# Raw tokens turned first, parameters loaded in two parts, other banks and another ScalarE order in attention, routing by column halves, and a last norm that ScalarE shares

## What is computed

```python
def hybrid_layer(x, ...):                      # first block, two layers
    h = rmsnorm(x, g_pre_mix)
    proj = h @ w_in                            # 16 pieces: heads of four kinds
    o_a = dsa_attention(...)                   # top 64 keys by an indexer
    o_b = forgetting_attention(...)            # decay by cumulated log gates
    o_c = differential_attention(...)          # lam = exp(lq1.lk1)-exp(lq2.lk2)+init
    o_d = sliding_window_sink_attention(...)
    x = x + rmsnorm(mix @ w_out, g_post_mix)
    m = jnp.square(jax.nn.relu(rmsnorm(x, g_pre_mlp) @ w_up)) @ w_down
    x = x + rmsnorm(m, g_post_mlp)
    return x + jax.nn.sigmoid(x @ w_ple_gate) * (p_i @ w_ple_proj)
```

## Time and profile before

| quantity | value |
|---|---|
| median of the three runs | 2034.21 us |
| the profiled execution | 2033.9 us |
| its span | 2032.1 us |
| busy PE / VectorE / ScalarE / GpSimd | 1988.8 / 1584.7 / 1210.5 / 96.9 us |
| share of PE in the chain that ended last | 93% |
| mean rate of the DMA queues | 237 GB/s |

### The profile page before, as it was taken

How to read it: one execution, slowest core, us unless ns; L and a number is a source line. 1 busy time by engine, 2 the same in 40 slices (tenths; PEclk the granted TensorE clock), 3 DMA queues, 4 the chain that set the end, 5 groups by cost and what they waited for, 6 DMA issues and landing times.

```text
span 2032.1 us, 30372 instructions
## 1 busy us (share of the span) xinstructions
PE 1988.8 (98%) x11719; PEld 1683.8 (83%) x11719; DVE 1584.7 (78%) x1636; ACT 1210.5 (60%) x1293; POOL 96.9 (5%) x162
## 2 busy tenths in 40 slices
PE   8999999999999999999999999999999999999996
PEld 7778888877888888888889888888888888888885
DVE  7777754778774469785458968989899999999998
ACT  5565534556554356544335636777777777777774
POOL 0310000031000000000000000000000000000000
PEclk9999999999999999999999999999999999999998
DMA  8316555532555554165556308999999999999994
GB/s 295 130 53 204 193 197 189 202 119 69 202 187 188 200 197 150 40 199 186 180 170 205 125 2 328 362 359 368 361 369 360 362 368 360 367 366 364 365 362 179
DMA packets 154216, 481.58 MB, mean 237 GB/s; under 512 B 14616, under 2 KB 41728, under 8 KB 153984
## 3 DMA queue, kind: packets, MB, share of 16 engines
q1 hardware_dynamic: 150048, 465.45, 63.8%
q0 software_dynamic: 4064, 14.68, 2.1%
HBM read 478.00 MB, written 2.10 MB: 236 GB/s over the span
## 4 chain that ended last, share of the span: by engine, by line
PE 93%; DVE 4%; ACT 1%; issue 1%; DMA 1%; POOL 0%; SPq 0%; DVEq 0%; POOLq 0%
PE G L673 18%; PE G L675 18%; PE G L674 18%; PE Sp L673 5%; PE Sp L675 5%; PE Sp L674 5%; PE G L1114 3%; PE G L700 3%; PE G L660 2%; PE G L1115 2%; PE G L655 1%; PE G L656 1%; PE Sp L1114 1%; PE G L1492 1%; DVE e_lo L2821 1%; PE G L978 1%
## 5 line engine op out<-in xcount | busy, mean ns | idle before, releaser
L1999 ACT ACTIVATE e_hi<-e_raw 128x1408 fp32r<-128x1408 f32 x384 | 524.1, 1381 | 154.7 <-DMA e_raw<-in_moe_w_gate 57.6
L2821 DVE TENSOR_TENSOR e_lo<-e_raw,e_hi 128x1408 fp32r<-128x1408 f32 x384 | 601.7, 1619 | 18.3 <-ACT e_hi L1999 15.5
L2071 DVE TENSOR_TENSOR ring_lo<-ring,ring_hi 128x2048 fp32r<-128x2048 f32 (+2 forms) x171 | 383.4, 2253 | 184.1 <-ACT ring_hi L1579 182.7
L1579 ACT ACTIVATE ring_hi<-ring 128x2048 fp32r<-128x2048 f32 (+1 forms) x179 | 335.4, 1882 | 228.6 <-PE G L675 132.2
L673 PE MATMUL G<-e_hi,xgTh 128*128 128x512 f32 (+1 forms) x768 | 289.5, 377 | 0.1
L675 PE MATMUL G<-e_hi,xgTl 128*128 128x512 f32 (+1 forms) x768 | 288.5, 376 | 0.0
L674 PE MATMUL G<-e_lo,xgTh 128*128 128x512 f32 (+1 forms) x768 | 286.9, 374 | 0.0
L673 PE MATMUL G<-ring_hi,xT 128*128 128x512 f32 (+2 forms) x500 | 195.7, 391 | 0.0
L675 PE MATMUL G<-ring_hi,xT 128*128 128x512 f32 (+2 forms) x500 | 192.1, 384 | 0.0
L674 PE MATMUL G<-ring_lo,xT 128*128 128x512 f32 (+2 forms) x500 | 191.9, 384 | 0.0
L674 PEld LDWEIGHTS G<-e_lo,xgTh 128*128 128x128 f32 x768 | 144.3, 188 | 23.8
(11 more groups left out here) (433 smaller groups left out, 3351.5 us busy)
## 6 DMA issues: line engine op xcount, KB each, us to landing
e_raw<-in_moe_w_gate SPq DMA_DIRECT2D x128, 704.0 KB, 6.0
e_raw<-in_moe_w_up SPq DMA_DIRECT2D x128, 704.0 KB, 6.0
e_raw<-in_moe_w_down SPq DMA_DIRECT2D x128, 704.0 KB, 6.0
ring<-in_w_in SPq DMA_DIRECT2D x48, 1024.0 KB, 5.1
ring<-in_w_mlp_up SPq DMA_DIRECT2D x32, 1024.0 KB, 5.2
ring<-in_w_mlp_down SPq DMA_DIRECT2D x32, 1024.0 KB, 4.8
ring<-in_w_out SPq DMA_DIRECT2D x16, 1024.0 KB, 4.9
ring<-in_ffn_w_gate SPq DMA_DIRECT2D x22, 512.0 KB, 3.8
```

The lines of the kernel that those rows point to most:

```text
L1579: nc.scalar.activation(ring_hi[:, n % H, 0:m], ring[:, n % R, 0:m], ACT.Copy).then_inc(w_hi.sem, 1)
L1999: nc.scalar.activation(e_hi[:, u, :], e_raw[:, u, :], ACT.Copy).then_inc(w_hi.sem, 1)
L2071: v.tensor_tensor(ring_lo[:, n % R, cs], ring[:, n % R, cs], ring_hi[:, n % H, cs].bitcast(F32), ALU.subtract).then_inc(w_lo.sem, 1)
L2821: v.tensor_tensor(e_lo[:, u, :], e_raw[:, u, :], e_hi[:, u, :].bitcast(F32), ALU.subtract).then_inc(w_lo.sem, 1)
```

## The change

Start. The raw tokens are turned as soon as they are there; the gain comes as eight rows of 128, is turned by PE to a column for each of the eight groups of features, and VectorE multiplies the turned tokens by it from PSUM (`gained`). ScalarE takes the high part of that product. The scale by the root is applied where ScalarE copies the columns of the input product. The turns are 6 and 14 instead of 30 and 10; the squares and the angles of the rotations stand later. SP's order becomes: tables, gain rows, block 0, four ring tiles, block 1, positions, the fifth. The gain after the mixer is loaded when four tiles are used. The small parameters come in two parts, at the sixth and at the eighth tile, and the rest of the tables at the tenth.

```diff
-        sp.dma_start(POS[:, :], ...)
-        for tb in range(NTB):
-            sp.dma_start(X[:, tb, :], ...)
+        sp.dma_start(GAIN8, w["norm_pre_mix"][0].rearrange("(k p) -> k p", p=P)).then_inc(gain_loaded.sem, 16)
+        sp.dma_start(X[:, 0, :], ...)
         for n, use in enumerate(TILES):
+            if n == LEAD:
+                sp.dma_start(X[:, 1, :], ...)
+                sp.dma_start(POS[:, :], ...)
             if n == R:
                 small_parameters()
+            if n == R + 2:
+                later_parameters()
+            if n == R + 4:
                 sp.dma_start(C[:, c1:], const_d[:, c1:]).then_inc(c_loaded[1].sem, 16)
...
+                pe.transpose(G[:, 1, 0:KT], GAIN8, ident[0:KT, 0:KT]).then_inc(gain_turned.sem, 1)
+                turns(6, G[:, 3, :])
+                token_transposes(X, 0, x_raw)
+                turns(14, G[:, 3, :])
+                first_cols(X, x_raw, [512, 512], ("act",), NTB, ahead=2)
...
-                    last = nc.scalar.activation(PROJ[:, tb, n0:n1], src[...], ACT.Copy)
+                    last = nc.scalar.activation(PROJ[:, tb, n0:n1], src[...], ACT.Copy, scale=1.0 if l else rstd[:, tb:tb + 1])
...
+                gained(0)
+                s_rstd.next("dve", NTB)
+                low_parts(LEAD - 1)
+                gained(1)
+                low_parts(LEAD)
                 angles()
-                pre_norm(0, VEC[:, 1, :])
-                low_evac(0, ...)
-                pre_norm(1, VEC[:, 1, :])
-                low_evac(1, ...)
-                low_parts(LEAD - 1)
-                block_evac(1)
-                low_parts(LEAD)
                 rotations()
...
-        gains(1, "norm_pre_mix", 0)
+        pool.wait_ge(w_used.sem, LEAD)
         gains(0, "norm_post_mix", 0)
```

```diff
     def half_bank(tb, half):
-        return G[:, 1, :] if tb == 1 and half == 1 else T[0]
+        return T[0] if half == 0 else G[:, 1, :] if tb else Sp[:, 0, :]
...
                 if u == 5:
+                    out_rows(1, 0, range(2))
                     output_transposes(0, 0)
-                    out_rows(1, 0)
+                    out_rows(1, 0, range(2, 4))
                 if u in (6, 7):
-                    if u == 6:
-                        bank_free_t(0)
...
-                values(u)
+                values(u, probs_taken)
                 if u == 2:
+                    rotated_transposes(QK_C, 1, c_rotated, Sp[:, 0, :])
                     last_columns(2, 1)
-                    rotated_transposes(QK_C, 1, c_rotated)
-                    bank_free_t(0)
```

```diff
+            for h in range(2):                     # last_product, block 1
+                for j in range(LEAD):
+                    if h and j == 1:
+                        tail()
+                    last = part(slots[j], j, 1, (h, h + 2), product)
+                if h == 0:
+                    last.then_inc(g_quarter.sem, 1)
...
-                pe.wait_ge(hb_ready.sem, hb_ready.seen["pe"] + 1)
...
+        def x_half(tb):
+            turns(3, Sp[:, 1, :])
+            x_block(tb)
+        token_transposes(X, 1, x_half)
+        for i in range(2):
+            turns(3, Sp[:, 1, :])
+            pe.wait_ge(x_hi[i].sem, n_x[i])
+            route(1, range(4 * i, 4 * i + 4), False)
+        turns(3, Sp[:, 1, :])
...
+        for tb in range(NTB):                      # ScalarE, last norm
+            nc.scalar.activation(..., ACC[:, tb, :], ACT.Identity, scale=-1.0 / D, accum_out=mv[:, tb, 0:1])
+            nc.scalar.activation(..., ACC[:, tb, :], ACT.Square, bias=mv[:, tb, 0:1], accum_out=mv[:, tb, 1:2])
...
+        for tb in range(NTB):                      # VectorE
+            for h in range(2):
+                added(tb, h)
+        centred_out(0)
         finished(0, slice(0, D))
+        centred_out(1)
```

More of the change, by code:

```diff
@@ L720, in cols_tile @@
             for k in groups:
-                last = product(G[:, bank, 0:width], xTh[:, 4 * j + k, toks], xTl[:, 4 * j + k, toks], bh[:, k, :], bl[:, k, :],
+                last = product(dst[:, bank, 0:width], xTh[:, 4 * j + k, toks], xTl[:, 4 * j + k, toks], bh[:, k, :], bl[:, k, :],
                                j == 0 and k == 0, j == 1 and k == 3)
@@ L879, in head_transposes, with rotated_transposes @@
                            act_takes=i == 0)
-            def rotated_transposes(first, tb, s):
+            def rotated_transposes(first, tb, s, bank=None):
                 pe.wait_ge(s.sem, NTB * l + tb + 1)
-                transposes(0, [(T[0][:, k * P:(k + 1) * P], head_source(first + k, tb)) for k in range(4)], act_takes=True)
+                dst = T[0] if bank is None else bank
+                transposes(0, [(dst[:, k * P:(k + 1) * P], head_source(first + k, tb)) for k in range(4)], act_takes=True, other=bank is not None)
             def index_dots(r):
@@ L1008, in output_transposes @@
                 bank = half_bank(tb, half)
-                other = tb == 1 and half == 1
+                other = half == 1
                 kept = t_free[0]
@@ L1686, in columns_taken @@
                 for n0, n1 in IN_CHUNKS[i]:
-                    last = nc.scalar.activation(PROJ[:, tb, n0:n1], src[:, c0:c0 + n1 - n0], ACT.Copy)
+                    last = nc.scalar.activation(PROJ[:, tb, n0:n1], src[:, c0:c0 + n1 - n0], ACT.Copy, scale=1.0 if l else rstd[:, tb:tb + 1])
                     c0 += n1 - n0
@@ L1744, in _ @@
             heads_evac(QKT[:, QK_C:QK_C + 4, 0:P])
+            nc.scalar.activation(warm[:, l:l + 1], c("one"), ACT.Exp)
             heads_evac(QKT[:, QK_D:QK_D + 4, 0:P])
@@ L2374, in _ @@
                     maxima(u + 2)
+                if u < 5:
+                    out(u)
                 if u + 1 < NU:
@@ L3069, in _ @@
                 expert_pool(i)
-        layer_norm(f_r, f_p)
+        for tb in range(NTB):
+            pool.wait_ge(f_sq.sem, tb + 1)
+            step(pool, g.tensor_scalar(ms[:, tb:tb + 1], mv[:, tb, 1:2], 1.0 / D, 1e-5, ALU.mult, ALU.add), pstep)
+            power(rstd[:, tb:tb + 1], ms[:, tb:tb + 1], 1, f_p)
     ctx.close()
```

207 lines of the change are left out of this document (143 added, 64 removed).

## The result

The changed kernel takes **2015.23 us** (median of four, 2014.38 to 2017.29) beside 2034.21 before: a ratio of 0.9907, with an interval of 0.9893 to 0.992. The forecast was 2015.2, in a range from 2009.5 to 2021. The total is right. The start's gain needed an edit that I had priced at nothing, attention and the last norm fell short, and a dip of the clock in the kernel before made up for it. The execution that is profiled took 2014.65 us, with a span of 2012.8.

What follows compares the result with a forecast made beforehand. TensorE was busy 1988.8 of 2032.1 us, so edits could only take from its 43 us of idle time. Gains 2.5 + 10.6 + 1.2 + 1.0 + 3.4 = 18.7 off 2033.9 gave 2015.2, range 2009.5 to 2021.

Steps and rivals of the forecast that it cites:

- Start: Kernel start: third ring tile lands 3 to 4.4 us earlier, but DVE becomes the bound; gain 2.5 us (1.5 to 4.4).
- parameters in two parts: Start: router rows issued later land near 38.2, before DVE's lambda sums near 38.9; worth 0, at worst 1 us.
- Attention: Both attention layers: 6.95 us of PE stalls each, DVE takes part back; gain 5.3 a layer, 10.6 in all.
- Dense SwiGLU: Dense SwiGLU: the down product needn't wait for G with the last chunk in Sp; gain 1.2 us (0 to 1.3).
- routing: Mixer's last product and routing, layer 1: half the sum and one stats move before the product's end; 1.0 us (0.3 to 1.8).
- Last norm: Kernel's end: half sums follow PE's pairs, ACT and POOL share DVE's work; gain 3.4 us (2.4 to 4).
- roots POOL's 0.24 + 0.58: Last norm: each block's root on POOL takes 0.24 + 0.58 us, with DVE's centring hidden beside them.
- The experts: Expert stage: as before, no gain or loss in the sum.
- VectorE taking more or less: Start and attention: DVE takes back more of PE's lead (2019.8) or less (2010.0); chance 0.13 each.
- The clock at the start: Start: with fewer turns the first eight products run at double spacing; 0.5 us lost, 2015.7; chance 0.03.
- The slower case: Start: router rows landing after more than 10 us hold DVE's lambda sums, each further us costing one; chance 0.04.

Runs made afterwards that it cites:

- late: Changed kernel with the second part of the parameters loaded two ring tiles later, at the tenth: 2023.31 us.
- the parameters together: Changed kernel with all thirteen parameters and the second part of the tables loaded at the sixth tile again: 2017.14 us.
- the first of the two last versions: Changed kernel with angles in front, positions behind the first tokens, gate norm parameters four tiles later, last centring in four pieces: 2015.74 us.
- the old order: Changed kernel with ScalarE's and VectorE's previous order in attention, keeping the new banks and the `warm` exponential: 2017.78 us.
- the run with the early angles: Changed kernel with positions loaded ahead of the first tokens and angles made while VectorE waits for the turned tokens: 2015.03 us.

## Why the prediction was right, and where only its sum was

- **Start, 2.5 forecast, 2.7 measured.** The copy into COLS comes at 46.91 (forecast near 47), and VectorE has no idle row between 20 us and that copy but one of 0.6 at the sine:

```profile
27.33 0.26 DVE L2310 TENSOR_TENSOR ARENA<-ARENA 128x96 f32<-128x96 f32 x1 [0.60 <-ACT ARENA L1770]
...
38.80 0.48 DVE L2321 TENSOR_TENSOR SM<-SM 128x64 f32<-128x64 f32 x2
...
46.91 0.26 DVE L2384 COPY COLS<-G 128x104 f32<-128x104 f32 x1
```

  That VectorE takes back a part of PE's lead is right: PE leads by 3.88 before that copy and by 2.66 behind it. But I credited this gain to the tokens and priced the **parameters in two parts at 0, at worst 1 us**. That step failed: without the split 1.5 us of the 2.7 are gone, and 2.9 with the dip. I had followed the router rows to the engine that waits for them, and not the sixth ring tile behind the tables: its landing at 36 us cost VectorE 0.22 us before, and costs it 1.68 once PE leads by 3.9. With the split its high part starts at 30.54.
- **Attention, 10.6 forecast, 10.1 measured.** Stalls gone, and VectorE named as what limits the rest: both shown. PE's waits for ScalarE's evacuations are 0.7 us a layer, as forecast under 1.5, and short ones for VectorE (0.5 us a layer or less) stand in their place. The give-back was a little larger than my sum: 5.0 and 5.1 instead of 5.3. VectorE's gaps in the window of 26 us fell from 3.0 to 1.3 and not to nothing.
- **Dense SwiGLU, 1.2 forecast, 1.1 measured**, and **routing, 1.0 forecast, 1.2 measured**: right in place and size.
- **Last norm, 3.4 forecast, 3.0 measured.** The step that failed is "roots POOL's 0.24 + 0.58": taken from the start, where VectorE was idle. Beside VectorE's centring, which I had called hidden, the second root took 1.18 + 0.55, some 0.9 us more with the gaps between, while the squares ahead of it came 0.4 earlier than forecast. The trace of the kernel before had the price already, in the second root of the start, beside VectorE's passes of 0.75:

```profile
9.97 0.74 POOL L2923 TENSOR_SCALAR SM<-SM 128x1 f32<-128x1 f32 x1 [0.21 <-ACT XN L1621]
10.79 1.05 POOL L2919 TENSOR_TENSOR SM<-SM,C 128x1 f32<-128x1 f32 x1
```

- **The experts, 0 forecast, -0.3 measured**; open.
- **Not in the sum: the clock dips.** The profiled execution of the kernel before holds one of 1.5 us, that of the changed kernel none. My terms come to 18.1 against 18.7 forecast; with the dip's 1.5, less the 0.3 of the experts, it is 19.3. The median's 19.0 is so near the forecast because terms that were 0.6 short in sum met this one, of which I knew nothing. That part is luck.
- **Rivals.** VectorE taking more or less (2019.8, 2010.0): neither. The clock at the start: its mechanism is real (1.0 us without turns, I had 0.5) but the changed kernel's turns prevent it. The slower case is real as well. Its margin is 1.3 us, where my estimates of the landing (38.2) and of VectorE (38.9) left 0.7. I had each us beyond cost one; in *late* 7.0 beyond cost 9.25, as the clock fell in the wait and PE waited for the row parameters too.

## What to carry to other kernels

When an edit brings a stage forward, look for the transfers whose landing does not come forward with it, and price their place in the queue against the new schedule: here a ring tile behind 1.2 MB of tables cost PE nothing before and would have taken back half of the start's gain. Bring large transfers behind the ring tiles that an engine asks for within the next 10 us, and small ones that a whole queue waits for ahead of them. When PE waits have been taken out one engine at a time, read the share of the next engine in that window: VectorE at 22.7 of 24.0 us named the next limit, and PE's last 1.0 us of idle time there is about what lifting it gave (1.2). When one run undoes everything and two others undo a half each, list what neither half takes back: here the 1.0 us that was missing was the `warm` exponential, and not an interplay.

## What the runs showed of the hardware

- The granted clock fell to 0.50 in stretches of 3.4 to 10.2 us in seven of the profiles while PE had work, and in an eighth over its last products. They began in or behind waits of PE (7.6 us in the late-parameter run, 2.4 with the parameters together, 2.2 in the first of the two last versions, 1.7 in the kernel before, run again, at its start, 0.7 with the old order), or among short products and turns. The same kernel had them in other places in two executions. A wait can therefore cost more than itself: 2.2 us more behind one of 7.6, 1.4 behind one of 2.4, and nothing behind the 1.7 of the changed kernel.
- TensorE's first products start at half rate (every 0.43 us) after eight transposes and a pause of 2.6 us, and at full rate (0.23) after eight transposes and 20 turns; the granted clock shows 1.00 in both.
- A 1 KB load of positions put behind the first tokens (first of the two last versions) and not ahead (the run with the early angles) landed at 5.68 us instead of 3.69, and the first ring tile behind it at 9.82 instead of 8.40; why so small a transfer moves a ring tile by 1.4 us, no run here tells.
- A small GpSimd instruction on 128x1 values that takes 0.2 us alone took 1.18 us beside a VectorE pass of 1.28 on 1024 columns, ending 0.05 us behind it, and 1.92 beside one of 2.29 at the changed kernel's start (22.67 us).
